# Gated one-hot rows of the dense-gate stage made by GpSimd between its row fetches, where ScalarE made them

## The reference

```python
def peer_ffn(h, w_q, sub_keys, u_tab, v_tab):
    ...
    experts = jnp.take_along_axis(cand, pick, axis=-1)
    gates = jax.nn.softmax(best, axis=-1)
    ...
    def expert_block(args):
        hb, eb, gb = args
        act = jax.nn.gelu(jnp.einsum('td,thkd->thk', hb, u_tab[eb]).astype(f32), approximate=False)
        return jnp.einsum('thk,thkd->td', (gb * act).astype(hb.dtype), v_tab[eb])
```

## Time and profile before

| | |
|---|---|
| median of 3 runs | 2312.95 us (2312.63 to 2314.08) |
| profiled execution | 2312.89 us |
| its span | 2311.1 us |
| busy TensorE, VectorE, ScalarE, GpSimd | 2227.0, 1755.5, 1122.6, 1050.8 us |
| matmuls of the gate products | from 1278.7 to 1611.4 us of the span |

### The profile page before, as it was taken

One profiled execution on the slowest core, in us unless ns is written; L12 is line 12 of the kernel. 1 busy time (PEld: TensorE's weight loads), 2 busy tenths in 40 slices (PEclk: granted clock), 3 DMA queues, 4 the chain that ended last, 5 costly groups with the idle time before them and its releaser, 6 DMA issues.

```text
span 2311.1 us, 43747 instructions
## 1 busy us (share of the span) xinstructions
PE 2227.0 (96%) x14976; PEld 2150.3 (93%) x14976; DVE 1755.5 (76%) x3436; ACT 1122.6 (49%) x2154; POOL 1050.8 (45%) x604
## 2 busy tenths in 40 slices
PE   7999889999999999999999999999999999999997
PEld 7999769999889999999999999999999999999996
DVE  8985685445648325888999988888578989899996
ACT  6554784456652213433434877878333333333332
POOL 3333365445444433344656544444534444544442
PEclk9999999999999999999999999999999999999998
DMA  3322345433125323234445899999999999999994
GB/s 129 116 83 81 127 154 201 157 124 116 59 73 155 103 86 127 93 127 146 145 143 202 294 328 330 334 336 359 375 369 394 393 386 393 389 388 383 384 385 146
DMA packets 225642, 526.50 MB, mean 228 GB/s; under 512 B 23792, under 2 KB 117072, under 8 KB 225376
## 3 DMA queue, kind: packets, MB, share of 16 engines
q1 hardware_dynamic: 144384, 284.47, 35.4%
q0 software_dynamic: 46240, 167.89, 19.8%
q10 hardware_dynamic: 34912, 72.78, 8.5%
HBM read 453.44 MB, written 72.80 MB: 228 GB/s over the span
## 4 chain that ended last, share of the span: by engine, by line
PE 64%; issue 17%; ACT 8%; POOL 6%; ACTq 2%; DVE 1%; DMA 1%; POOLq 0%; SPq 0%; DVEq 0%
PE ps L1473 24%; PE ps L877 17%; PE ps L1342 8%; POOL wlo L736 5%; PE ps L1058 4%; PE ps L1097 3%; ACT rinv L2041 2%; ACT whi L1568 2%; ACT g_block L2066 1%; ACT onehot_i L2045 1%; PE ps L1041 1%; PE ps L1428 1%; PE ps L1235 1%; ACT tmp L1983 1%; PE ps L1204 1%
## 5 line engine op out<-in xcount | busy, mean ns | idle before, releaser
L736 POOL TENSOR_TENSOR wlo<-raw,whi 128x1024 fp32r<-128x1024 f32 x179 | 456.0, 2548 | 597.9 <-ACT whi L1568 597.8
L1568 ACT ACTIVATE whi<-raw 128x1024 fp32r<-128x1024 f32 x373 | 394.1, 1057 | 675.7 <-PE ps L1473 214.3
L1342 PE MATMUL ps<-h_hi,whi 128*128 128x416 f32 x1008 | 359.8, 357 | 17.7 <-DVE wlo L2879 10.7
L748 POOL DMA_INDIRECT row<-pu,row_idx x160 | 230.1, 1438 | 291.6 <-DVE row L2870 213.6
L1473 PE MATMUL ps<-act_hi,whi 128*128 128x416 f32 x1000 | 351.1, 351 | 3.4 <-DVE act_lo L2941 3.4
L1342 PE MATMUL ps<-h_lo,whi 128*128 128x416 f32 x1008 | 353.3, 351 | 0.0
L1342 PE MATMUL ps<-h_hi,wlo 128*128 128x416 f32 x1008 | 353.2, 350 | 0.0
L1473 PE MATMUL ps<-act_lo,whi 128*128 128x416 f32 x1000 | 351.1, 351 | 0.0
L1473 PE MATMUL ps<-act_hi,wlo 128*128 128x416 f32 x1000 | 350.9, 351 | 0.0
L748 POOL DMA_INDIRECT row<-pv,row_idx x160 | 232.3, 1452 | 245.4 <-DVE row_acc L2928 177.8
L2879 DVE TENSOR_TENSOR wlo<-raw,whi 128x1024 fp32r<-128x1024 f32 x194 | 236.9, 1221 | 90.5 <-ACT whi L1568 89.5
(11 more groups left out here) (410 smaller groups left out, 4731.1 us busy)
## 6 DMA issues: line engine op xcount, KB each, us to landing
raw<-wt SPq DMA_DIRECT2D x245, 512.0 KB, 3.5
raw<-pv SPq DMA_DIRECT2D x128, 512.0 KB, 9.4
activations<-tmp ACTq DMA_DIRECT2D x128, 208.0 KB, 4.2
gates_dense<-g_block ACTq DMA_DIRECT2D x52, 512.0 KB, 6.7
g_tiles<-gates_dense SPq DMA_DIRECT2D x32, 832.0 KB, 9.3
gelu<-activations SPq DMA_DIRECT2D x128, 208.0 KB, 10.7
a_cum_rows<-decay_sums SPq DMA_DIRECT2D x32, 256.0 KB, 3.3
state_s<-s_in SPq DMA_DIRECT2D x16, 512.0 KB, 7.6
```

The source lines that it names most:

```text
L736: pool.tensor_tensor(lo, raw[n.par][:, :], hi.bitcast(F32), ALU.subtract).then_inc(split_ready, 1)
L748: pool.indirect_dma_start(GR[b][:, :], None, table[:, :], bass.IndirectOffsetOnAxis(ap=IDX[:, s:s + 1], axis=0))\
L1342: mm = pe.matmul(PS[2 * p.par][:, 0:DT], w[slot][:, k, :], x[:, k, 0:DT], start=k == 0 and w is whi and x is HH, stop=k == KD - 1 and w is ...
L1568: act.activation(whi[slot][:, :, :].rearrange("p k c -> p (k c)"), raw[n.par if n.b < N_V else slot][:, :], ACT.Copy)\
```

## The change

`hots` moves from ScalarE to GpSimd. For each quad GpSimd makes `AI` of tokens 2 and 3 by one comparison and product each, as VectorE does for tokens 0 and 1, and signals `hot_act`. Turn 0 is made ahead of the stage's first DMA; those of turn t + 1 stand in turn t among the row fetches: two quads, two fetches, two quads, two fetches. Each quad waits for `g_ready` of turn t. ScalarE loses both instructions of each such token. `EJT`'s negative gates are no longer needed, and VectorE loses their four instructions.

```diff
-ACT_HOTS = SU + TURNS * QUADS
+ACT_HOTS = SU
...
+            def hots(t, k):
+
+                if t:
+                    pool.wait_ge(g_ready, (t - 1) * QUADS + k + 1)
+                for x in range(2):
+                    tok = t * 16 + 4 * k + 2 + x
+                    ins = pool.tensor_scalar(AI[k][:, 2 + x, :], iota, EJT[:, 0, tok:tok + 1], EJT[:, 2, tok:tok + 1],
+                                             ALU.is_equal, ALU.mult)
+                ins.then_inc(hot_act, 1)
+
+            pool.wait_ge(routed, CHUNKS)
+            for k in range(QUADS):
+                hots(0, k)
             pool.wait_ge(parts_ready, CHUNKS)
...
             for t in range(TURNS):
-                for x in range(TURN_ROWS[t]):
-                    rows(RING + sum(TURN_ROWS[:t]) + x)
+                for x in range(4):
+                    if x % 2 == 0 and t < TURNS - 1:
+                        for y in range(2):
+                            hots(t + 1, x + y)
+                    if x < TURN_ROWS[t]:
+                        rows(RING + sum(TURN_ROWS[:t]) + x)
...
-            def hots(t, k):
-
-                dist = [RINV[:, (2 * (k % 2) + x) * P:(2 * (k % 2) + x + 1) * P] for x in range(2)]
-                tok = [bass.ds(t * 16 + (4 * k + 2 + x), 1) for x in range(2)]
-                for x in range(2):
-                    ins = act.activation(dist[x], iota, ACT.Square, bias=EJT[:, 0, tok[x]], scale=-1.0)
-                ins.then_inc(act_own, 1)
-                act.wait_ge(act_own, t * QUADS + (SU + k + 1))
-                for x in range(2):
-                    ins = act.activation(AI[k][:, 2 + x, :], dist[x], ACT.Relu, bias=EJT[:, 2, tok[x]],
-                                         scale=EJT[:, 3, tok[x]])
-                ins.then_inc(hot_act, 1)
-
-            act.wait_ge(routed, CHUNKS)
-            for k in range(QUADS):
-                hots(0, k)
...
-                        if not last or t < BTURNS - 1:
-                            hots(b * BTURNS + (t + 1), k)
...
-                own.mark(dve.tensor_scalar(EJT[:, 3, bass.ds(t0, L)], PS[7][:, 2 * P:2 * P + L], -1.0, None,
-                                           ALU.mult))
...
-                own.enter(c, 1, 65)
+                own.enter(c, 1, 64)
```

## The result

The changed kernel is **slower by 4%**: 2406.46 us median (2403.26 to 2414.32, 4 runs) beside 2313.51 us for the kernel before (2312.63 to 2314.22, 4 runs), a ratio of 1.0407 with an interval of 1.0384 to 1.043. The forecast was 2301 us in a range of 2294 to 2330, so time and sign were both wrong. The profiled execution took 2414.32 us, with a span of 2412.5.

A forecast was written before the change was run, and what follows sets the result against it. ScalarE's list was taken to set the gate stage's pace. Fifty half-turns going from 6.68 to 6.43 us give 12.5 us, less 0.5 for start-up: 12 us off 2312.89, so 2301 us, range 2294 to 2330.

The forecast's parts named there:

- What bounds the kernel now: Gate stage: ScalarE's list, not TensorE's, sets the pace in half the half-turns; 18.8 us lost, 6.68 us against 6.30.
- TensorE alone: Rival for the gate stage: blockades fall into VectorE's idle time, 18 us gained, 2295 us; chance 0.15.
- What is removed: ScalarE's squares, relus and own waits in the gate stage: 3.4 us a half-turn, so `high` no longer comes late.
- GpSimd's price: Each of GpSimd's 208 new 128 x 128 instructions was taken at 0.4 us, between 0.22 and 0.615.
- GpSimd's time: GpSimd's list in the gate stage: 3.1 us for fetches and gaps plus 4 x 0.4, so 4.7 us a half-turn.
- What it takes from VectorE: GpSimd's four instructions delay VectorE by 0.2 us each, raising its half-turn from 5.53 to 6.33 us.
- the blockade: VectorE's two-input instructions and GpSimd's SBUF-reading ones exclude each other; taken as 0.2 us lost on VectorE per GpSimd instruction.
- GpSimd becomes the bound: Rival: each GpSimd instruction lets one of VectorE's pass, 0.63 us; 7.2 us a half-turn, 2339 us; chance 0.07.
- What is moved: Row fetches now stand behind `hots` on GpSimd; in time by 2.7 us, at the longest landing 1.4 late, costing nothing.
- Turn 0's eight instructions: GpSimd's first instructions, ahead of its `parts_ready` DMA: 4.8 us, claimed just hidden before the first gate product at 1278.7.
- "Wrong" signs: Profile signs against the forecast: GpSimd instruction over 0.6 us, VectorE comparisons of 0.8 us, TensorE or VectorE waiting for rows.

The follow-up runs named there:

- e1: Changed kernel with GpSimd making the gated one-hot rows of tokens 2 and 3 for turn 0 only, never again: 2295.74 us.
- e6: Changed kernel with GpSimd's comparisons replaced by memsets of the same rows, same places and waits: 2292.57 us.
- e7: Kernel before, with VectorE making three of each quad's four tokens, ScalarE one, GpSimd only its fetches: 2295.58 us, ratio 0.9918.
- e5: Kernel before plus eight extra GpSimd instructions on scratch tiles at its start, while VectorE idles, to price them: 2309.31 us in one run.
- e9: Changed kernel with each GpSimd comparison replaced by a 128-column copy that still reads SBUF: 2300.61 us.
- e2: Changed kernel with each two row fetches put ahead of the comparisons of their half-turn: 2408.02 us.
- e3: Changed kernel with the gate stage's row dots on VectorE cut from 1024 to 128 columns: 2331.4 us.

## Why the prediction was wrong, step by step

- **What bounds the kernel now: right.** ScalarE's list set the pace, and with it unloaded TensorE's floor of 6.30 us a half-turn shows (e1, T = 6.42 and 2295.74 us; e6, 6.33; e7, 6.36). "TensorE alone" was reckoned at 2295.
- **What is removed: right.** ScalarE is busy for 31% of the stretch; VectorE's wait for `high` is down to 2.9 us there, but VectorE is late itself; the better sign is e1, where VectorE still waits 28.8 us for `high`, ScalarE in turn waits 138.1 us for TensorE's tiles, and TensorE never stops.
- **GpSimd's price: wrong.** Taken as 0.4 us between 0.22 and 0.615; it is 0.785 (e5; the minimum in the changed kernel is 0.780). The upper bound was a product of two tensors, as the dearer thing; the comparison with two scalars is dearer. That makes 4 x 0.785 = 3.1 us a half-turn instead of 1.6. On paper this alone would have cost little: with the 3.1 us for fetches GpSimd's list would have 6.2 us, just under TensorE's 6.30. No run has the price without the wait.
- **GpSimd's time, "if nothing holds it up": this is the step that failed.** It was entered as 4.7 us without any wait. In the changed kernel a comparison waits (1.384 + 0.010 - 0.785 =) 0.61 us on average, 2.4 us a half-turn. 3.1 + 2.4 + 2.8 for the fetches and their gaps (117.5 us in the 41.75 half-turns that 167 comparisons are) and 0.1 for the other DMAs make 8.4 us, the 8.42 measured behind the opening. The wait does its harm together with the price: e9's copy waits 0.45 us but takes only 0.28 of its own, and its 2300.61 us are what was forecast for the comparison.
- **What it takes from VectorE: nearly absent, since the blockade goes the other way.** The sum charged VectorE 0.8 us a half-turn. VectorE's comparisons in the changed kernel and its `low`:

```profile
L2856 DVE TENSOR_SCALAR onehot_i<-consts_sb,expert_turned 128x128 f32<-128x128 f32 x164 | 55.9, 383 | 0.0
L2875 DVE TENSOR_TENSOR wlo<-raw,whi 128x1024 fp32r<-128x1024 f32 x41 | 50.0, 1220 | 3.0 <-ACT whi L1585 2.9
```

  A comparison takes 383 ns, `low` 1220 as in the earlier trace rows, a dot 1244: some 4 x 0.04 + 2 x 0.03 = 0.2 us a half-turn. (In the kernel before a comparison took 340 ns in the mean and a dot 1219.) The earlier trace rows showed both sides of the conflict: GpSimd's subtraction lengthened from 2.40 to 3.31 us, and VectorE's instruction to 2.77. The subtraction beside the comparison at 1271.26 was lengthened too, to 2.84 us (from 1270.76 in that trace), where the prediction has 2.40. The prediction carried only VectorE's loss into the sum. It also took it from a GpSimd instruction of 1024 columns, whereas here GpSimd's are short and VectorE's are the long ones in an unbroken row.

  The Trainium skill (SBUF — State Buffer, § Who interferes with whom) lets a VectorE instruction with two SBUF inputs contend with a GpSimd instruction that reads SBUF, and not with one that only writes it. The trace agrees: 0.205 us for a memset, 1.38 for a comparison in the same place. Of VectorE's two-port modes the Trainium skill says in that section that whoever issues first gets the shared pair for the whole instruction and the other is blocked; if two-input instructions do the same, a comparison waits for one VectorE instruction, 1.22 us at most, and the 3.67 us above show more.
- **The rival "GpSimd becomes the bound" was the mechanism**, at a chance of 0.07 and 2339 us. Its wait of 0.63 us an instruction is near the measured mean of 0.61, in part by luck: it let each comparison wait for one VectorE instruction, and half of them wait for hardly anything while others wait up to 3.0 us. Its price of 0.4 was not right. With 0.785 it gives 3.1 + 4 x (0.785 + 0.63) = 8.76 us and 2417. The argument against it, that a late GpSimd would slide beside VectorE's short comparisons, failed: `OJ` and `low` and the dots, all with two inputs, take 204 of the 350 us, and the ten comparisons that start beside one of VectorE's own wait 1.34 us on average.
- **What is moved: right that order costs nothing** (e2), though the rows did come late in the changed kernel, as a consequence of GpSimd's lateness. The DMA share of 0.97 to which e1 went did no harm. **Turn 0's eight instructions, "just hidden" at 4.8 us, were not:** GpSimd's list in the changed kernel shows them behind the first product of 1281.0:

```profile
1277.01 11.97 POOL L846 TENSOR_SCALAR onehot_i<-consts_sb,expert_turned 128x128 f32<-128x128 f32 x8
```

  e1 keeps these eight, and its first up tile starts 11.2 us after the first gate product, where it is 6.6 in e6; that is why its T is 6.42 and not e6's 6.33.
- **"Wrong" signs:** three of those named are there, a GpSimd instruction over 0.6 us, VectorE waiting for rows (the 111.1 us above), and TensorE waiting for GpSimd's one-hot rows, though not in each half-turn (28.6 us in 18 waits, 3.6 at the longest, between 1300 and 1650 us); comparisons on VectorE of 0.8 us are not the rule (0.38 on average).

What stays open: why a comparison gets in after one, two or three of VectorE's instructions, and why a copy never waits for more than about one; a long instruction that does not read, which would part length from reading, was not tried. e3 shortens the dots alone; what `low` and `OJ` cost stands only in the list by starts above, without a run that shortens them.

## What to carry to other kernels

Before work goes to GpSimd, price the very instruction there (its scalars and its two operations), and add the wait that it will have behind the two-input instructions of VectorE: here 0.79 us alone became 1.38, and 1.82 where VectorE was 86% busy. GpSimd's 43% in the stage did not show what room it had: an instruction that only writes fitted (e6, 2292.57 us), a short one that reads just fitted (e9, 2300.61), the comparison did not. One comparison a quad more on VectorE itself, at some 0.26 us, was the cheap place (e7, 2295.58 us). And a large wait on an engine with time to spare, like the 111 us for rows, is not the cause until an edit that removes it moves the time.

## What the runs showed of the hardware

- GpSimd's instruction waited behind three VectorE instructions in a row, 3.67 us instead of 0.78, while VectorE lost less than 0.1 us.
- GpSimd's comparison and product with two scalars for each partition costs 3.4 ns a column and some 0.36 us besides (e5). A copy costs (1.032 - 0.29) / 896 = 0.83 ns a column (the earlier trace rows and e5), so it is the operations and the scalars that make a column dear. The Trainium skill (GPSIMD Engine Reference, § 4.1) calls operations of one input roughly line-rate there; the run does not agree for this one, since VectorE does two of them in 0.59 us, and GpSimd two in 1.59.
- TensorE's granted clock fell in the stage, from 1.00 to 0.91. TensorE in order of time behind the 3.67 us shown above, and two stretches of 4 us:

```profile
1398.72 1.99 PE L1445 MATMUL ps<-onehot_i,onehot_j 128*128 128x128 f32 x8 [2.74 <-POOL onehot_i L846]
1400.36 0.69 PE L1359 MATMUL ps<-h_hi,whi 128*128 128x416 f32 x1
1400.85 0.55 PE L1359 MATMUL ps<-h_lo,whi 128*128 128x416 f32 x1
1401.20 0.55 PE L1359 MATMUL ps<-h_hi,wlo 128*128 128x416 f32 x1
1401.54 0.55 PE L1359 MATMUL ps<-h_hi,whi 128*128 128x416 f32 x1
```

```profile
1400.00:1404.00 4.00, 4.00 (x19) 3.90 (x18) 1.84 (x4) 0.60 (x1) 3.96 (x5) 0.72 0.87 285
1404.00:1408.00 4.00, 4.00 (x30) 3.99 (x29) 4.00 (x9) 1.46 (x2) 3.53 (x3) 1.00 0.33 128
```

  After 2.74 us of idling the matmuls start 0.34 to 0.35 us apart, at the lower level of 1.2 GHz, where 24 of them take 4.52 us, 0.19 apart, at 2.4. In the second stretch the clock is back at 1.00, with 30 matmuls in 4 us instead of 19. GpSimd hardly ever waits for TensorE here, so this lies beside its list; what it would cost by itself was not measured.
